# Third layer of a fused fp32 network: rotary key columns as a narrow fp32 product in column quarters, and a first group of two key units and a query unit

## The chip, the cores and the metric

The kernel runs on one core of a Trainium2 chip, as one launch. The metric is device time in microseconds (us) of one execution. Engines are named as the profile names them: PE (TensorE matmul), PEld (its weight load), DVE (VectorE), ACT (ScalarE), POOL (GpSimd), SP (SyncE, which issues nearly all loads).

## The reference, cut to what matters

Three transformer-like layers over 256 latent and 256 context tokens of width 1024, all in fp32. The change lies in the mixer of the third layer, a latent attention. Its projections are:

```
c_q, c_kv, k_pe = split(h @ w_in, [768, 768 + 256])        # w_in: 1024 x 1056
q  = (rms_norm(c_q, q_norm_w) @ w_uq).reshape(b, l, 16, 64 + 32)
kv = (rms_norm(c_kv, kv_norm_w) @ w_ukv).reshape(b, l, 16, 64 + 64)
k_pe = apply_rope_2(k_pe[:, :, None, :], cos, sin)          # latent tokens only
k  = concatenate([k_nope, broadcast_to(k_pe, (b, l, 16, 32))], -1)
```

`c_kv` (256 columns) and `k_pe` (32 columns, the rotary key, the same for all 16 heads) are needed for all 512 tokens, `c_q` (768 columns) for the 256 latent tokens alone. `h` is the modulated norm of the layer's input.

## The kernel before, in words

**Weights.** Weights stream through three slots as units; a unit of this stage is 128 output columns by 1024 inputs (8 blocks k of 128), 512 KB. SP loads it into `raw` (L502; the slot must have been split by POOL), ACT rounds it to fp32r in `w_hi` (L1466; the products of the unit three before must be done), POOL writes the rest `raw - w_hi` to `w_lo` in two halves (L2010). A product of an fp32 weight and an fp32 input is then three fp32r matmuls: high by high, high by low, low by high (`three`, L584 to L586). The list of phases (`weight_phases`) fixes the order of units, steps and banks for every engine; each engine walks it by its own program and waits on counters: `rounded`, `split`, `steps` (PE finished a unit), `taken` (a result was read, so that its PSUM bank is free; the banks rotate over three).

**The third layer's start.** DVE and ACT make `h` block by block: DVE scales (L2230), ACT shifts and rounds (`h_hi`, L1539, counter `h_round`), DVE writes the rest (`h_lo`, L2239, counter `h_split`). Phase `ckv` has three units: two of `c_kv` and a third that holds the 32 rotary columns four times over, so that they fill 128. `linear(..., gate, early=True)` runs the three units side by side over blocks 0 to 3, those products that need only `h_hi` first (L767, L768), the rest after `h_split` (L772), then each unit alone over blocks 4 to 7 (L584 to L586). All have 512 token columns.

**Then.** Phase `cq`: six units with 256 token columns, `high_then_low` (L731, L732, then L737). After its first unit PE waits for `lk_in` and sums the squares of `c_kv` (L1348): ACT squared both key units (L1934), DVE scaled them (L2971) and added the squares (`std`, L2975). After its third unit PE spreads the inverse (L1354). DVE copies the rotary unit to `kpe` (L2103), and turns the latent half with shuffle, two multiplications and an addition (L2979 to L2982). Beside units 1, 2, 4 and 5 of `cq` ACT copies `kpe` to four of the sixteen heads each (L1959). DVE splits `ckv` into high and low (L2106), counter `lk_done`, for which PE waits before phase `uk`: two units of 512 columns by 256 inputs, eight products of six matmuls, each read by two copies of DVE (L2103). Phases `uv` (eight products) and `uq` (twelve units) follow, then attention.

Of the kernel before, what the change touches and what calls it, by code (L numbers as in the profile page):

```python
# [9 lines left out]
F32 = mybir.dt.float32  # L10
# [3 lines left out]
P = 128  # L14
D = 1024
KD = D // P
CTX = LAT = 256
TOK = CTX + LAT
# [20 lines left out]
LQ = LN + LR  # L39
# [96 lines left out]
def weight_phases():  # L136
    out = []

    def ffn(n):
        out.append(Phase(f"up{n}", 2 * KF, KD * P))  # L140
        out.append(Phase(f"down{n}", 3 * KD, SLOT, parts=3))

    out.append(Phase("va_gates", 2, LEAD + KD // 2 * 144))
    out.append(Phase("ka", 1, KD * P))
    out.append(Phase("qa", 4, KD * P))
    out.append(Phase("vma", 2, KD * P, 2, 2))
    out.append(Phase("km", 4, KD * P))
    out.append(Phase("vmb", 2, KD * P, 2, 2))
    out.append(Phase("qm", 4, KD * P))
    out.append(Phase("om", 4, KD * P))  # L150
    out.append(Phase("out0", 8, KD * P))
    ffn(0)
    out.append(Phase("in1", 24, KD * P))
    out.append(Phase("vra", 3, 272, ranges=((0, 3), (3, 6), (6, 8))))
    out.append(Phase("vrb", 2, KD * P, 2, 2))
    out.append(Phase("out1", 8, KD * P))
    ffn(1)
    out.append(Phase("ckv", 3, KD * P))
    out.append(Phase("cq", 6, KD * P))
    out.append(Phase("uk", 2, 2 * 512, 4, 4))  # L160
    out.append(Phase("uv", 2, 2 * 512, TT, TT))
    out.append(Phase("uq", 12, 6 * P))
    out.append(Phase("out2", 8, KD * P))
    ffn(2)
    unit = step = taken = 0
    ada = 16
    for f in out:
        f.every, f.number = CARRIED.get(f.name, (1, 0))
        f.first_ada, f.carry = ada, CARRY.get(f.name, f.units)
        ada += f.carry // f.every * f.number  # L170
        f.first_unit, f.first_step, f.first_taken = unit, step, taken
# [18 lines left out]
def build(nc, dram, small_at, tables_at, layers=3):  # L190
# [4 lines left out]
    with ExitStack() as stack:  # L195
# [296 lines left out]
        @block.sync  # L492
        def _(sp):
            sp.dma_start(small[:, :], dram["small"]).then_inc(s["small_in"], 16)

            def load(g):

                f, u = all_units[g]
                if g >= SLOTS:
                    f0, u0 = all_units[g - SLOTS]  # L500
                    sp.wait_ge(s["split"], 2 * (f0.first_unit + u0 + 1))
                sp.dma_start(raw_slot(f, u), source(f, u)).then_inc(full[g % SLOTS], 16)  # L502
                if g >= SLOTS and f0.every < SLOTS:
                    load_carried(f0, u0)
                if f.every >= SLOTS:
                    load_carried(f, u)

            def load_ada(k):

                if k - 16 >= SLOTS:  # L510
                    sp.wait_ge(s["ada_sum"], sums_after[k - SLOTS + 1])
                sp.dma_start(ada_w[:, k % SLOTS, :], dram[f"ada{k // 48}"][k % 48]).then_inc(ada_full[k % SLOTS], 16)

            def load_carried(f, u):

# [12 lines left out]
            sp.dma_start(X[:, :, 0:L0], dram["ctx"]).then_inc(s["x_in"], 16)  # L528
            sp.dma_start(fixed[:, :], dram["table3"]).then_inc(s["fixed_in"], 16)
            load_first_ada(3, 8)  # L530
            g = 0
            for name in run:
                f = ph[name]
                if name == "qm":

                    sp.wait_ge(s["cond_ready"], 1)
                    sp.dma_start(cond[:, :, :], dram["cond1"]).then_inc(s["cond_in"], 16)
                for u in range(f.units):
                    load(g)
                    if g == 1:  # L540
                        load_first_ada(8, 16)
                    if g == 2:
                        sp.dma_start(room0, dram["table0"]).then_inc(s["tables_in"], 16)
                        sp.dma_start(cond[:, 0, :], dram["cond0"][:, 0, :]).then_inc(s["cond_in"], 16)
                    g += 1

            if layers < 3:
                sp.wait_ge(s["x_ready"], 1)
                if layers == 2:
                    sp.wait_ge(s["taken"], ph["ckv"].first_taken)  # L550
                sp.dma_start(dram["out"], X[:, :, L0:L1]).then_inc(s["out_done"], 16)
                sp.wait_ge(s["out_done"], 16)
            else:
                for n, a in ((0, 2), (1, 4), (None, 0), (2, 6)):
                    if n is None:
                        sp.wait_ge(s["pool_scaled"], 4)
                    else:
                        sp.wait_ge(s["x_ready"], 2 + n)
                    sp.dma_start(dram["out"][:, a:a + 2, :], X[:, a:a + 2, L0:L1]).then_inc(s["out_done"], 16)
                sp.wait_ge(s["out_done"], 64)  # L560
# [3 lines left out]
        def _(pe):  # L564
# [778 lines left out]
            def latent_keys(u):  # L1343
# [7 lines left out]
                if u == 2:  # L1351
# [3 lines left out]
                                         ident, start=True, stop=True)  # L1355
                    last.then_inc(s["lk_spread"], 1)

            def latent_queries():
                pe.wait_ge(s["lq_in"], 1)
                for i in range(2):  # L1360
                    last = pe.matmul(bank[7][:, i:i + 1], sq_sum[:, i * P:(i + 1) * P], ones[:, 0:1],
                                     start=True, stop=True)
                last.then_inc(s["lq_sum"], 1)
# [47 lines left out]
            if layers == 2:  # L1411
                return
            feature_sums(0, TOK, "ckv")
            linear("ckv", 0, TOK, gate=next_h(), early=True)
            linear("cq", L0, L1, after=latent_keys)
            pe.wait_ge(s["lk_done"], 1)

            f = ph["uk"]
# [31 lines left out]
        def _(act):  # L1450
# [486 lines left out]
            def query_parts(u):  # L1937
# [13 lines left out]
                if u == 3:  # L1951
                    for i in range(2):
                        act.wait_ge(s["lk_work"], i + 1)
                        act.activation(ckv_hi[:, i, :], ckv[:, i, :], ACT.Copy).then_inc(s["lk_hi"], 1)
                if u == 1:
                    act.wait_ge(s["kpe_in"], 1)
                if u in (1, 2, 4, 5):
                    q = (1, 2, 4, 5).index(u)
                    act.activation(kh[LN:LQ, 4 * q:4 * q + 4, :], kpe[LN:LQ, :].unsqueeze(1).to_broadcast([LR, 4, TOK]),  # L1959
                                   ACT.Copy).then_inc(s["kpe_done"], 1)  # L1960

# [19 lines left out]

            phase("ckv", key_squares)
            phase("cq", query_parts)
            phase("uk", query_scale)
            phase("uv")
            phase("uq", spread_queries)
            attention(att2, 2 * AH, LH, LQ ** -0.5, False)
            out_and_squares("out2", L0, L1)
# [107 lines left out]
        def _(dve):  # L2096
# [868 lines left out]
            def mixer2():  # L2965
                def keys(p, b):

                    if p == 2:
                        return copy(kpe[LN:LQ, :], b[LN:LQ, :])
                    dve.wait_ge(s["lk_sq"], p + 1)  # L2970
                    return dve.tensor_scalar(ckv[:, p, :], b[:, :], S("kv_norm")[:, p:p + 1], None, ALU.mult)  # L2971

                each_product("ckv", keys)
                taken("cq")
                dve.tensor_tensor(std[:, :], work[:, 0, :], work[:, 1, :], ALU.add).then_inc(s["lk_in"], 1)  # L2975
                dve.wait_ge(s["tables_in"], 48)
                cs, sn = (C2(x) for x in ("cos", "sin"))
                k_lat, k_swap = kpe[LN:LQ, L0:L1], kswap[LN:LQ, :]
                then(dve.stream_shuffle(k_swap, k_lat, swap16))  # L2979
                dve.tensor_tensor(k_lat, k_lat, cs[LN:LQ, :], ALU.mult)  # L2980
                then(dve.tensor_tensor(k_swap, k_swap, sn[LN:LQ, :], ALU.mult))
                dve.tensor_tensor(k_lat, k_lat, k_swap, ALU.add).then_inc(s["kpe_in"], 1)  # L2982

                def queries(p, b):

# [31 lines left out]
                    if p == 0:  # L3017
                        last.then_inc(s["taken"], 1)
                dve.wait_ge(s["lq_lo"], 6)
                taken("uk")  # L3020
                dve.nop().then_inc(s["lq_in"], 1)

                def plain_keys(p, b):

# [158 lines left out]
def _layout(i):  # L3183
# [42 lines left out]
        arrays[f"up{n + 1}"] = _units(_pairs(i["w_ffn_gate_2"][n], i["w_ffn_up_2"][n]), P)  # L3226
        arrays[f"down{n + 1}"] = _units(i["w_ffn_down_2"][n], P)
    arrays["cq"] = _units(w2[:, :768], P)
    arrays["ckv"] = _units(np.concatenate([w2[:, 768:1024], np.tile(w2[:, 1024:], (1, 4))], 1), P)
    uq = np.asarray(i["mla_w_uq_2"][0]).reshape(768, LH, LQ)  # L3230
    arrays["uq"] = _units(np.concatenate([uq[:, :, LN:].reshape(768, -1), uq[:, :, :LN].reshape(768, -1)], 1), P)
    ukv = np.asarray(i["mla_w_ukv_2"][0]).reshape(256, LH, LN + LV)
# [27 lines left out]
```

## Time and profile before

| | us |
|---|---|
| median of 3 runs | 1456.79 |
| lowest, highest | 1455.14, 1459.68 |
| span of the profiled execution | 1454.6 |

The profiled execution's own time is given by its span, from the first instruction to the last. In the profile's page each engine has a line of busy time; a view of stretches gives busy time and granted clock by stage; a timeline gives each instruction's start and duration, with the idle time before it and what ended it. Ends of matmuls are modelled, so the time that one costs in a stream is read from start to start.

### The profile page before, as it was taken

To read this page: it belongs to the slowest core of one execution; us is meant where nothing else is said; L and a number is where in the kernel's file an instruction comes from. 1 tells how busy PE (TensorE), PEld (TensorE's weight loads), DVE (VectorE), ACT (ScalarE), POOL (GpSimd) and SP (SyncE) were. 2 spreads that over 40 slices of the span, in tenths; PEclk is the share of its full clock that TensorE was granted. 3 is DMA by queue.
4 is the path that set the end of the run, shared out by engine and by line. 5 is a ranking of instruction groups with operands and counts; after the bars stand their busy time and mean duration, and the time that the engine had idled before them with its cause. 6 is when DMAs were issued, how large, how long until landed. Compare 5 with 4: busy or idle time off the path is not lost.

```text
span 1454.6 us, 21621 instructions
## 1 busy us (share of the span) xinstructions
PE 1403.6 (96%) x8272; PEld 1172.3 (81%) x8272; DVE 848.5 (58%) x1638; ACT 659.0 (45%) x1070; POOL 840.2 (58%) x672
## 2 busy tenths in 40 slices
PE   5999999999999999999999999999999999999998
PEld 2978789999988888546878888888888866888887
DVE  3798667776676689688675333321126768554522
ACT  3555665455453133684342232232226386544442
POOL 1533427998864444675444554544446530699997
PEclk9999999999999999999999999999999999999999
DMA  9748516777775652010445555533333320365664
GB/s 365 288 164 309 195 50 212 248 258 241 243 259 194 202 192 80 31 44 15 174 174 182 195 202 185 193 122 96 102 107 102 110 94 16 118 200 188 187 187 135
DMA packets 71207, 242.01 MB, mean 166 GB/s; under 512 B 7488, under 2 KB 12992, under 8 KB 70720
## 3 DMA queue, kind: packets, MB, share of 16 engines
q1 hardware_dynamic: 68688, 236.63, 48.1%
q10 hardware_dynamic: 2416, 4.00, 0.9%
q8 instruction: 66, 1.08, 0.3%
q14 instruction: 37, 0.30, 0.1%
HBM read 238.50 MB, written 1.05 MB: 165 GB/s over the span
## 4 chain that ended last, share of the span: by engine, by line
PE 52%; DVE 4%; ACT 1%; issue 0%; POOL 0%; DVEq 0%; ACTq 0%
PE bank L731 9%; PE bank L737 9%; PE bank L732 9%; PE bank L593 8%; PE bank L594 4%; PE bank L584 2%; PE bank L586 1%; PE bank L585 1%; PE bank L592 1%; PE cond_a L1124 1%; PE bank L1124 1%; DVE h_both L2239 1%; PE bank L1132 1%; PE cond_a L1185 1%; PE bank L1144 1%; PE cond_b L1144 1%
## 5 line engine op out<-in xcount | busy, mean ns | idle before, releaser
L2010 POOL TENSOR_TENSOR w_lo<-raw,w_hi 128x512 fp32r<-128x512 f32 (+2 forms) x610 | 776.8, 1302 | 581.1 <-ACT w_hi L1466 572.9
L1466 ACT ACTIVATE w_hi<-raw 128x1024 fp32r<-128x1024 f32 (+3 forms) x300 | 307.9, 1029 | 582.7 <-PE bank L737 375.2
L731 PE MATMUL bank<-h_both,w_hi 128*128 128x512 f32 (+1 forms) x1000 | 323.1, 340 | 1.2 <-ACT w_hi L1466 1.2
L732 PE MATMUL bank<-h_both,w_hi 128*128 128x512 f32 (+1 forms) x1000 | 322.5, 340 | 0.0
L731 PEld LDWEIGHTS bank<-h_both,w_hi 128*128 128x128 f32 x1000 | 188.3, 188 | 22.9 <-ACT w_hi L1466 1.4
L732 PEld LDWEIGHTS bank<-h_both,w_hi 128*128 128x128 f32 x1000 | 188.3, 188 | 21.3
L737 PE MATMUL bank<-h_both,w_lo 128*128 128x512 f32 (+1 forms) x1000 | 198.1, 340 | 0.0
L737 PEld LDWEIGHTS bank<-h_both,w_lo 128*128 128x128 f32 x1000 | 160.4, 188 | 21.4 <-POOL w_lo L2010 0.2
L2124 DVE CUSTOM_DVE_ANT_0 ada_junk<-ada_w,cond_a 128x1024 bf16<-128x1024 f32 x128 | 153.5, 1215 | 15.1 <-DVE work L2687 8.1
L2106 DVE TENSOR_TENSOR hidden_both<-work,hidden_both 128x256 fp32r<-128x256 f32 (+1 forms) x66 | 58.5, 886 | 135.0 <-ACT hidden_both L1547 135.0
L593 PE MATMUL bank<-h_both,w_hi 128*128 128x512 f32 x345 | 122.8, 394 | 0.0
L2674 DVE SCALAR_TENSOR_TENSOR X<-bank,mod,X 128x256 f32<-128x256 f32 x64 | 29.3, 480 | 141.5 <-PE bank L737 123.4
L731 PE MATMUL bank<-hidden_both,w_hi 128*128 128x256 f32 (+1 forms) x330 | 102.7, 331 | 0.0
L732 PE MATMUL bank<-hidden_both,w_hi 128*128 128x256 f32 (+1 forms) x330 | 102.6, 331 | 0.0
L594 PE MATMUL bank<-h_both,w_lo 128*128 128x256 f32 x345 | 96.5, 280 | 0.0
L2124 DVE CUSTOM_DVE_ANT_0 ada_junk<-ada_w,cond_b 128x1024 bf16<-128x1024 f32 x64 | 77.8, 1215 | 0.0
L593 PEld LDWEIGHTS bank<-h_both,w_hi 128*128 128x128 f32 x345 | 64.8, 188 | 13.3 <-issue 0.4
L584 PE MATMUL bank<-h_both,w_hi 128*128 128x256 f32 (+1 forms) x192 | 67.2, 350 | 3.8 <-DVE h_both L2239 1.8
L2103 DVE TENSOR_SCALAR arena<-bank 128x512 f32<-128x512 f32 (+3 forms) x65 | 38.7, 598 | 51.6 <-PE bank L737 33.5
L732 PEld LDWEIGHTS bank<-hidden_both,w_hi 128*128 128x128 f32 x330 | 62.1, 188 | 6.0
L731 PEld LDWEIGHTS bank<-hidden_both,w_hi 128*128 128x128 f32 x330 | 62.1, 188 | 6.0
L594 PEld LDWEIGHTS bank<-h_both,w_lo 128*128 128x128 f32 x345 | 64.9, 188 | 2.0
(487 smaller groups left out, 2544.1 us busy)
## 6 DMA issues: line engine op xcount, KB each, us to landing
raw<-in_up SPq DMA_DIRECT2D x132, 512.0 KB, 3.6
ada_w<-in_ada SPq DMA_DIRECT2D x128, 512.0 KB, 4.5
raw<-in_down SPq DMA_DIRECT2D x48, 448.0 KB, 3.5
raw<-in_out SPq DMA_DIRECT2D x24, 512.0 KB, 3.5
raw<-in_down SPq DMA_DIRECT2D x24, 512.0 KB, 3.6
raw<-in_in SPq DMA_DIRECT2D x24, 512.0 KB, 3.5
arena<-in_ada SPq DMA_DIRECT2D x16, 512.0 KB, 11.8
raw<-in_uq SPq DMA_DIRECT2D x12, 384.0 KB, 3.1
```

The source lines that it names most:

```text
L584: pe.matmul(out, w_h, x_h, start=first, stop=False)
L593: pe.matmul(out.rearrange("p (h n) -> p h n", h=2), w_h, x_both, start=first, stop=False)
L594: return pe.matmul(out[:, 0:LAT], w_l, x_both[:, 0], start=False, stop=False)
L731: pe.matmul(out, w_h[:, k - k0], hi[:, k, cols], start=(k == 0), stop=False)
L732: pe.matmul(out, w_h[:, k - k0], lo[:, k, cols], start=False, stop=False)
L737: last = pe.matmul(out, w_l[:, k - k0], hi[:, k, cols], start=False, stop=(k == K - 1))
L1466: act.activation(part_slot(w_hi, f, u), raw_slot(f, u), ACT.Copy).then_inc(s["rounded"], 1)
L2010: pool.tensor_tensor(part_slot(w_lo, f, u)[:, a:b], raw_slot(f, u)[:, a:b], part_slot(w_hi, f, u)[:, a:b].bitcast(F32), ALU.subtract).then ...
L2103: return dve.tensor_scalar(out, in_, 1.0, None, ALU.mult)
L2106: return dve.tensor_tensor(out, x, hi.bitcast(F32), ALU.subtract)
L2124: dve.tensor_tensor_reduce(ada_junk[:, ada_sums[0] % 2, :], ada_w[:, k % SLOTS, :], silu_c[m][:, :], 1.0, 0.0, ALU.mult, ALU.add, mod[:, n ...
L2674: last = dve.scalar_tensor_tensor(out=X[:, k, a:e], in0=b[:, a - t0:e - t0], scalar=mod[:, layer[0] % 2, 8 * chunk + k, m:m + 1], in1=X[:, ...
```

## The change

- The rotary columns leave phase `ckv` (now two units) and become a phase `kpe` of their own after `cq`: one unit of 1024 by 32, 128 KB. The number of units in all, and each unit's slot from `cq` on, stay: `cq` moves up one place, and `kpe` takes the place before `uk`.
- `latents_first` replaces `linear("ckv")` and the first unit of `cq`: the two key units (512 token columns) and the first query unit (256) run side by side over blocks 0 to 3, each block behind `h_split`, then each alone over blocks 4 to 7; after it `latent_keys(0)`, so the wait for `lk_in`.
- `rotary_keys`, after the last query unit: 32 matmuls in plain fp32 with the unrounded weight in `raw` and both parts of `h`. A result of 32 columns takes a quarter of the array; the four quarters hold context and latent tokens, each for blocks 0 to 3 and for blocks 4 to 7.
- DVE: the copy of the rotary unit and the rotation leave their place before the query units; behind the last query unit it makes four copies of 32x256 out of the bank, adds the halves, and rotates (`rotary_key`), before the copies of `uk`.
- ACT: the copies of `kpe` to the heads move from `cq` to `uv`, two to each of its two units.
- SP: the load of the unit three after `kpe` (the first of `uv`) waits also for the product of `kpe`, which reads `raw`.

```
-    out.append(Phase("ckv", 3, KD * P))
+    out.append(Phase("ckv", 2, KD * P))
     out.append(Phase("cq", 6, KD * P))
+    out.append(Phase("kpe", 1, KD * LR))
...
                     sp.wait_ge(s["split"], 2 * (f0.first_unit + u0 + 1))
+                    if f0.name == "kpe":
+                        sp.wait_ge(s["steps"], f0.steps_after(u0))
...
+            def latents_first(gate):
+                f, n = ph["ckv"], ph["ckv"].units + 1
+                slots = [[part_slot(x, f, u, KD) for x in (w_hi, w_lo)] for u in range(n)]
+                def one(u, k):
+                    t0 = 0 if u < f.units else L0
+                    return three(bank_of(f.first_taken + u)[:, 0:TOK - t0], *(w[:, k] for w in slots[u]),
+                                 h_hi[:, k, t0:], h_lo[:, k, t0:], k == 0, k == KD - 1)
+                for k in range(KD // 2):
+                    gate(k)
+                    for u in range(n):
...
+                        one(u, k)
+                for u in range(n):
+                    for k in range(KD // 2, KD):
+                        if u == 0:
+                            gate(k)
+                        last = one(u, k)
+                    last.then_inc(s["steps"], 1)
+                latent_keys(0)
+            def rotary_keys():
...
+                w = raw_slot(f, 0).rearrange("p (k n) -> p k n", k=KD)
+                for k in range(KD // 2):
+                    for x in (h_hi, h_lo):
+                        for g in range(4):
+                            j, t0 = g // 2 * KD // 2 + k, g % 2 * L0
+                            last = pe.matmul(bank_of(f.first_taken)[LR * g:LR * g + LR, 0:L0], w[:, j],
+                                             x[:, j, t0:t0 + L0].bitcast(F32), start=(k == 0 and x is h_hi),
+                                             stop=(k == KD // 2 - 1 and x is h_lo))
+                last.then_inc(s["steps"], 1)
...
-            linear("ckv", 0, TOK, gate=next_h(), early=True)
-            linear("cq", L0, L1, after=latent_keys)
+            latents_first(next_h())
+            linear("cq", L0, L1, after=latent_keys, first=1)
+            rotary_keys()
             pe.wait_ge(s["lk_done"], 1)
...
+            def spread_rotary_keys(u):
+                act.wait_ge(s["kpe_in"], 1)
+                for q in range(2 * u, 2 * u + 2):
                     act.activation(kh[LN:LQ, 4 * q:4 * q + 4, :], kpe[LN:LQ, :]...
...
+                def rotary_key():
...
+                    copy(kpe[LN:LQ, 0:L0], b[0:LR, 0:L0])
+                    copy(kpe[LN:LQ, L0:L1], b[LR:2 * LR, 0:L0])
+                    copy(rope_s[LN:LQ, 0, :], b[2 * LR:3 * LR, 0:L0])
+                    copy(rope_s[LN:LQ, 1, :], b[3 * LR:P, 0:L0]).then_inc(s["taken"], 1)
...
+                    dve.tensor_tensor(kpe[LN:LQ, 0:L0], kpe[LN:LQ, 0:L0], rope_s[LN:LQ, 0, :], ALU.add)
+                    then(dve.tensor_tensor(k_lat, k_lat, rope_s[LN:LQ, 1, :], ALU.add))
...
                 dve.wait_ge(s["lq_lo"], 6)
-                taken("uk")
+                taken("kpe")
                 dve.nop().then_inc(s["lq_in"], 1)
+                rotary_key()
```

## Rows read from the trace of the kernel before

**Rows 1.** The page: PE's busy time, share of the span and instructions.
```profile
PE 1403.6 (96%) x8272; PEld 1172.3 (81%) x8272; DVE 848.5 (58%) x1638; ACT 659.0 (45%) x1070; POOL 840.2 (58%) x672
```

**Rows 2.** The view of stretches, around the third layer's projections.
```profile
core 0: us, PE busy (x) PEld busy (x) DVE busy (x) ACT busy (x) POOL busy (x), PEclk, DMA share, GB/s
1107.85:1124.10 16.25, 16.25 (x138) 16.12 (x136) 10.18 (x15) 13.86 (x21) 13.55 (x11) 1.00 0.47 160
1125.30:1137.00 11.70, 11.66 (x50) 8.82 (x50) 10.72 (x17) 4.80 (x6) 6.40 (x5) 1.00 0.35 104
1137.30:1148.60 11.30, 11.30 (x50) 9.12 (x50) 7.58 (x14) 1.68 (x3) 3.98 (x4) 1.00 0.24 76
```

**Rows 3.** Timeline of PE: start, duration, what, idle time before and what ended it.
```profile
1087.40 0.50 PE L767 MATMUL bank<-h_both,w_hi 128*128 128x512 f32 x1 [0.33 <-ACT h_both L1539]
...
1099.51 0.40 PE L584 MATMUL bank<-h_both,w_hi 128*128 128x512 f32 x1
...
1104.97 0.28 PE L731 MATMUL bank<-h_both,w_hi 128*128 128x256 f32 x1
...
1107.85 0.95 PE L1348 MATMUL cond_a<-fixed,std 128*128 128x1 f32 x8
...
1123.05 1.12 PE L737 MATMUL bank<-h_both,w_lo 128*128 128x256 f32 x8
1125.34 0.50 PE L584 MATMUL bank<-ckv_hi,w_hi 128*128 128x512 f32 x1 [1.17 <-DVE ckv_lo L2106]
```

**Rows 4.** Timeline of DVE.
```profile
1087.38 0.88 DVE L2239 SCALAR_TENSOR_TENSOR h_both<-cond_b,mod,h_both 128x256 fp32r<-128x256 f32 x2
1096.79 1.87 DVE L2239 SCALAR_TENSOR_TENSOR h_both<-cond_b,mod,h_both 128x256 fp32r<-128x256 f32 x4
1104.16 0.75 DVE L2971 TENSOR_SCALAR spare<-bank,small 128x512 f32<-128x512 f32 x1 [1.96 <-ACT work L1934]
1105.90 0.85 DVE L2975 TENSOR_TENSOR std<-work 128x512 f32<-128x512 f32 x1
1106.78 0.45 DVE L2979 STREAM_SHUFFLE spare<-spare 32x256 f32<-32x256 f32 x1
1108.10 1.50 DVE L2981 TENSOR_TENSOR spare<-spare,arena 32x256 f32<-32x256 f32 x1
1127.66 0.51 DVE L3010 TENSOR_TENSOR sq_sum<-sq_sum,work 128x256 f32<-128x256 f32 x1
1128.34 11.33 DVE L2103 TENSOR_SCALAR arena<-bank 64x512 f32<-64x512 f32 x16 [0.18 <-DVE sq_sum L3010]
1151.02 0.42 DVE L3040 TENSOR_TENSOR spare<-bank,arena 128x256 f32<-128x256 f32 x1 [1.51 <-PE bank L737]
1151.36 0.41 DVE L3041 TENSOR_TENSOR spare<-bank,arena 128x256 f32<-128x256 f32 x1
```

**Rows 5.** Timeline of PE near the kernel's start: fp32 products in column quarters.
```profile
21.91 0.64 PE L661 MATMUL cond_b<-arena 128*32 128x256 f32 x8 [0.25 <-DMA arena<-in_ada]
32.44 1.08 PE L661 MATMUL cond_b<-arena 128*32 128x256 f32 x16
```

**Rows 6.** Timeline of ACT.
```profile
1102.51 1.06 ACT L1466 ACTIVATE w_hi<-raw 128x1024 fp32r<-128x1024 f32 x1 [1.20 <-PE bank L586]
1103.48 0.58 ACT L1934 ACTIVATE work<-bank 128x512 f32<-128x512 f32 x1
1113.60 1.91 ACT L1959 ACTIVATE arena<-spare 32x2048 f32<-32x2048 f32 x1
```

**Rows 7.** Timeline of POOL, and the page's row of a load.
```profile
1106.37 5.82 POOL L2010 TENSOR_TENSOR w_lo<-raw,w_hi 128x512 fp32r<-128x512 f32 x4 [0.17 <-ACT w_hi L1466]
1138.15 1.99 POOL L2010 TENSOR_TENSOR w_lo<-raw,w_hi 128x384 fp32r<-128x384 f32 x2 [2.92 <-ACT w_hi L1466]
...
raw<-in_uq SPq DMA_DIRECT2D x12, 384.0 KB, 3.1
```

**Rows 8.** The view of stretches, after an idle PE; then PE's timeline before one.
```profile
659.80:663.10 3.30, 3.30 (x13) 1.04 (x9) 3.27 (x7) 1.03 (x1) 3.30 (x4) 0.50 0.01 2
...
658.71 2.67 PE L1185 MATMUL bank<-arena,spare 128*64 128x512 f32 x8 [2.10 <-DVE arena L2900]
```

More of the change, by code:

```diff
@@ L1356, in latent_keys @@
                     last.then_inc(s["lk_spread"], 1)
+            def latents_first(gate):
[8 more added lines that the diff above has]
+                    for u in range(n):
+                        if k == 0:
+                            pe.wait_ge(s["split"], 2 * (f.first_unit + u + 1))
+                            room(f.first_taken + u)
+                        one(u, k)
[7 more added lines that the diff above has]
+            def rotary_keys():
+                f = ph["kpe"]
+                loaded(pe, f, 0)
+                room(f.first_taken)
+                w = raw_slot(f, 0).rearrange("p (k n) -> p k n", k=KD)
[7 more added lines that the diff above has]
+                last.then_inc(s["steps"], 1)
             def latent_queries():
@@ L1954, in query_parts @@
                         act.activation(ckv_hi[:, i, :], ckv[:, i, :], ACT.Copy).then_inc(s["lk_hi"], 1)
[L1955 to L1958, printed above, removed]
+            def spread_rotary_keys(u):
+                act.wait_ge(s["kpe_in"], 1)
+                for q in range(2 * u, 2 * u + 2):
                     act.activation(kh[LN:LQ, 4 * q:4 * q + 4, :], kpe[LN:LQ, :].unsqueeze(1).to_broadcast([LR, 4, TOK]),
@@ L1983, in _ @@
             phase("cq", query_parts)
+            phase("kpe")
             phase("uk", query_scale)
-            phase("uv")
+            phase("uv", spread_rotary_keys)
             phase("uq", spread_queries)
@@ L2966, in keys @@
                 def keys(p, b):
-                    if p == 2:
-                        return copy(kpe[LN:LQ, :], b[LN:LQ, :])
                     dve.wait_ge(s["lk_sq"], p + 1)
@@ L2975, in mixer2 @@
                 dve.tensor_tensor(std[:, :], work[:, 0, :], work[:, 1, :], ALU.add).then_inc(s["lk_in"], 1)
-                dve.wait_ge(s["tables_in"], 48)
-                cs, sn = (C2(x) for x in ("cos", "sin"))
[L2978 to L2982, printed above, removed]
+                def rotary_key():
+                    f = ph["kpe"]
+                    product_in(f, 0)
+                    b = bank_of(f.first_taken)
+                    copy(kpe[LN:LQ, 0:L0], b[0:LR, 0:L0])
+                    copy(kpe[LN:LQ, L0:L1], b[LR:2 * LR, 0:L0])
+                    copy(rope_s[LN:LQ, 0, :], b[2 * LR:3 * LR, 0:L0])
+                    copy(rope_s[LN:LQ, 1, :], b[3 * LR:P, 0:L0]).then_inc(s["taken"], 1)
+                    dve.wait_ge(s["taken"], f.first_taken + 1)
+                    k_lat, k_swap = kpe[LN:LQ, L0:L1], kswap[LN:LQ, :]
+                    dve.tensor_tensor(kpe[LN:LQ, 0:L0], kpe[LN:LQ, 0:L0], rope_s[LN:LQ, 0, :], ALU.add)
+                    then(dve.tensor_tensor(k_lat, k_lat, rope_s[LN:LQ, 1, :], ALU.add))
+                    dve.wait_ge(s["tables_in"], 48)
+                    then(dve.stream_shuffle(k_swap, k_lat, swap16))
+                    dve.tensor_tensor(k_lat, k_lat, cs[LN:LQ, :], ALU.mult)
+                    then(dve.tensor_tensor(k_swap, k_swap, sn[LN:LQ, :], ALU.mult))
+                    dve.tensor_tensor(k_lat, k_lat, k_swap, ALU.add).then_inc(s["kpe_in"], 1)
+                cs, sn = (C2(x) for x in ("cos", "sin"))
                 def queries(p, b):
@@ L3228, in _layout @@
     arrays["cq"] = _units(w2[:, :768], P)
-    arrays["ckv"] = _units(np.concatenate([w2[:, 768:1024], np.tile(w2[:, 1024:], (1, 4))], 1), P)
+    arrays["ckv"] = _units(w2[:, 768:1024], P)
+    arrays["kpe"] = _units(w2[:, 1024:], LR)
     uq = np.asarray(i["mla_w_uq_2"][0]).reshape(768, LH, LQ)
```

## The prediction

> **What bounds the kernel now.** I read the page first: PE is busy for 96% of the span [rows 1], so time is won by PE work removed or by its waits removed, and lost by new waits. Then the view of stretches, for the part that changes [rows 2]: in the query units PE is busy throughout, in the key products (`uk`) nearly so, at the full granted clock. Then the timeline of PE [rows 3], to see where each unit starts and the one real wait, 1.17 us before `uk` for DVE's `ckv_lo`; and those of DVE, ACT and POOL [rows 4, 6, 7], since a shorter PE path asks for their results earlier. What the reader should see there is that `uk` is already paced by DVE: its sixteen copies take 11.33 us [rows 4], 1.42 a product, while PE could do a product in 1.40: the 48 matmuls of the same width in `uv` take 11.3 us [rows 2], and the same number in `uk` takes 11.7.
>
> **The price of one matmul.** From 1099.51 to 1104.97 PE runs 24 matmuls of 512 columns, two half units [rows 3], so 0.2275 us each. From 1104.97 to 1107.85 it runs 24 of 256 columns, 0.120 each. A unit of `cq` costs 2.88, a unit with 512 columns 5.46.
>
> **Part 1, the first group.** It no longer starts on `h_hi` alone. Before, PE began at 1087.40 [rows 3]; now it waits for the first `h_lo`, at 1088.26 [rows 4]. A block of the new group costs 6 x 0.2275 + 3 x 0.120 = 1.725, four make 6.9, so PE is at 1095.2, then has 0.68 per block of the first unit. The last block's `h_lo` ends at 1096.79 + 1.87 = 1098.66 in both kernels [rows 4], and that sets the end of the first unit: about 1099.5 before and after. Cost 0; the cover is DVE's pace. If it were gone, the later start would cost 0.9.
>
> Then the second key unit's half, 12 x 0.2275 = 2.73, to 1102.24, and the query unit's half, 12 x 0.120 = 1.44, to 1103.68. Before, PE came to this point (the sums of L1348) at 1107.85 [rows 3]. So 4.17 us go: 2.73 of rotary work ahead of it, and 1.44 of the query unit that now hide behind `h`. (The rotary unit's other half, before, was in the shared stretch; it goes behind DVE's pace and frees nothing there.)
>
> **Part 2, what is late next.** The sums need `lk_in`. ACT rounds a unit when the second key unit is done, at 1102.51, then squares (done 1104.06) [rows 6]; DVE scales from 1104.16 for 0.75 [rows 4]; then, without the rotary copy that stood between, the addition of 0.85 ends at 1105.8. None of these can start earlier, since the second key unit ends when it did. PE therefore sits idle from 1103.7 to 1105.8, a new wait of 2.1 us, and of the 4.17 only 2.05 are kept. Behind that wait stand all other query units. They run on as before: 16.15 us from 1107.85 to 1124.0 [rows 2, 3], now 1105.8 to 1121.95. Weights are no bound there: ACT loses four copies of 1.91 [rows 6], 7.6 us of the 13.9 it was busy in this stretch, and POOL has a unit fewer to split.
>
> **Part 3, the narrow product.** The kernel has the same form at its start: four fp32 products of 128x256 into four column quarters are 8 records, and they take 0.64 us alone and 1.08 for two such sets [rows 5], so 0.44 a set and 0.20 for the tail. Here are 4 blocks x 2 parts = 8 sets: 3.52 us, to 1125.47, with a result at 1125.7. The wait for `lk_done` is gone by then: without ACT's copies and the rotation on DVE, `ckv_lo` follows the fourth query unit, at about 1119.4, and even at its 3.5 us is done by 1123. So `uk` may start at 1125.5, against 1125.34: PE's work is 5.46 less 3.52, but nearly all that is spent by the wait of part 2.
>
> **Part 4, DVE behind it.** The rotation now starts with the result, 1125.75, and DVE's copies of `uk` are queued behind it. An operation of this size with one operand in PSUM takes 0.42, started 0.34 after the one before [rows 4]: four copies are 1.44. The two additions, two multiplications and last addition are like the 0.51 of L3010, 0.40 where the next needn't wait: 2.3. The shuffle is 0.45 [rows 4], own waits some 0.2. Sum 4.4, so the first copy of `uk` starts at 1130.15 and not at 1128.34 [rows 4]: 1.8 later. With three banks PE's fourth product waits for DVE's first, so at 1125.5 + 4.2 PE stops for about 1.9, and from there both kernels go at DVE's 1.42 a product. `uk` ends 1.8 later.
>
> Bounds: at 0.34 for each of the ten operations and 0.45 for the shuffle it is 3.9 (and the shift 1.3); with the 1.50 of L2981 [rows 4] for the five that read two operands in SBUF, some 5 more. That row was measured beside POOL's 5.82 us of splitting [rows 7]. Here POOL is between jobs: its split of the second `uk` unit ends near 1126.2, and the next needs the load held back by part 5. I take the low end. The Trainium skill (SBUF — State Buffer, "Who interferes with whom") says the same as a rule: a DVE instruction with two SBUF inputs and a GpSimd instruction that reads SBUF exclude each other for their whole length. By it a meeting would cost up to 1.4 per instruction; the trace bears that out, and it is a rival below.
>
> **Part 5, the moved edges.** SP's load of the first `uv` unit waits for 1125.7; 3.6 us of DMA at most, 1.06 of ACT [rows 6], 2.6 of POOL: 1133, and `uv` starts at 1139. Behind it in SP's queue stands the second `uv` unit, needed 5.6 later still. Cost 0, cover 6 us. ACT's copies in `uv`: two after the first unit's rounding, two after the second's, 3.82 each, so ACT is free at about 1155.2 where its next rounding could start at 1152.7. PE wants that unit (the fourth of `uq`) at 1157.0, its low part at 1158.5; rounding gives 1156.1, POOL (1.99 a unit [rows 7]) 1158.1. From there load 3.1, rounding 0.85 and split 1.99 make 6.1 for three units where PE takes 6.4. Cost 0, but by a few tenths; if it fails, up to 1.
>
> **Sum.** -2.05 (kept of part 1) + 3.52 (product) - 1.34 (the old wait, 1124.0 to 1125.34) = +0.15 at the start of `uk`; in `uk` the shift of DVE's start decides: +1.8. The profiled execution would go from 1454.6 to 1456.4; the median of the runs shown is 2.2 above that span, so 1458.6.
>
> **The rivals.**
> - *The clock falls at the new wait.* The granted clock is 0.50, so 1.2 GHz of 2.4, over the 3.3 us from 659.8, and PE had been idle 2.10 just before [rows 8]; it did not fall behind the 1.17 before `uk` [rows 2, 3]. Now 2.1 idle is followed by 0.8 of one-column sums [rows 3]. Half speed for such a stretch is 1.65 more: 1460.3. The Trainium skill (TensorE: Matmul & The Clock Gate, "What's actually happening") has the clock halved by too little activity, and by that rule the trace agrees. Against: PE is full on both sides of the new wait, which it isn't around 659.8. Chance 18%.
> - *Not slower: DVE does not decide `uk`.* If copies and rotation behind the product fit in the 2.8 us that PE's first two products leave, PE runs `uk` in 11.2 from 1125.5 and loses nothing; it ends 0.3 earlier than before: 1456.5. It decides from a chain of 2.8 us down. Four copies alone are 1.44 and seven more steps would have to take 0.2 each; every row says more. A shorter wait in part 2 would help the same way. 13%.
> - *POOL meets the rotation.* Two or three blocked instructions, 1.0 each: +3, 1461.6. 8%.
> - *The change doesn't do what it says: the quarters run one after another.* 64 records at 0.22 are 14.1 instead of 3.5: 1469. The sets of [rows 5] speak against it, and the form is the same. 4%.
> - Forecast: 50%. The remaining 7% is anything else, of both signs.
>
> **How the numbers follow.** Time is that of the forecast, 1458.6, with its own range 1457 to 1460.5. Medians of three scatter by more than a microsecond (1455.14 to 1459.68 here); with the rivals the range is 1454.7 to 1462. 0.3%, about what a measurement of this kernel can tell from no change, is 4.4 us: forecast, clock and not-slower lie within it, so within 81%, slower 14% (quarters, half of the POOL case, part of the clock's), faster 5%: even the full 2.05 + 1.34 without any price for the product would be only 3.4.
>
> **What would show it.** An idle of about 2 us before L1348's sums, ended by DVE's `std`; 64 records of the narrow product in 3.7 us; no wait for `ckv_lo`; one wait of about 1.9 in `uk` before its fourth product, with DVE's rotation ahead of its first copy; no idle in `uq`. Wrong if the wait in `uk` is missing, if the sums start before 1105, or if `uq` shows gaps.

## The result, and the profile after

Nine executions of each kernel: the changed one takes 1464.07 us (median, 1460.51 to 1466.35), the one before 1456.79 (1451.40 to 1460.30). The ratio is 1.0047 with a 95% interval of 1.0034 to 1.0059: slower by 0.47%, about 7 us, where I forecast 1.8 and a range up to 1462. Two executions of all that follow, one of before at 1990 us and one of the kernel of experiment 4 at 7876 us, stand far apart from the rest and enter no ratio. The profiled execution has a span of 1462.8, 8.2 more than before. Line numbers have moved: L1351 is what L1348 was, L587 to L589 were L584 to L586, L734, L735 and L740 were L731, L732 and L737.

Timeline of PE after (start, duration, what, idle before it and what ended it):

```profile
1089.07 0.50 PE L587 MATMUL bank<-h_both,w_hi 128*128 128x512 f32 x1 [1.24 <-DVE h_both L2285]
...
1107.52 1.87 PE L1351 MATMUL cond_a<-fixed,std 128*128 128x1 f32 x8 [2.90 <-DVE std L3019]
...
1126.81 3.66 PE L1396 MATMUL bank<-h_both,raw 128*32 128x256 f32 x64
1130.40 0.50 PE L587 MATMUL bank<-ckv_hi,w_hi 128*128 128x512 f32 x1
...
1136.23 0.50 PE L587 MATMUL bank<-ckv_hi,w_hi 128*128 128x512 f32 x1 [1.38 <-DVE arena L2149]
...
1186.52 0.66 PE L1135 MATMUL bank<-fixed,arena 128*128 128x128 f32 x4 [2.30 <-DVE arena L2630]
```

Four places answer to the four steps forecast. There is a new wait before the sums (2.90, not 2.1); the narrow product is 64 records in 3.66; the wait before `uk` [rows 3] is gone; and a wait of 1.38 stands before the fourth product of `uk`. But the sums themselves take 1.87 where they took 0.95 [rows 3]. The view of stretches says why:

```profile
core 0: us, PE busy (x) PEld busy (x) DVE busy (x) ACT busy (x) POOL busy (x), PEclk, DMA share, GB/s
1103.90:1107.10 3.20, 0.72 (x7) 0.52 (x5) 2.13 (x2) 2.52 (x5) 2.99 (x4) 1.00 0.46 148
1107.30:1114.00 6.70, 6.48 (x30) 6.48 (x31) 0.56 (x2) 0.17 (x1) 2.52 (x2) 0.50 0.33 102
1114.20:1126.80 12.60, 12.60 (x107) 12.47 (x105) 6.34 (x13) 7.18 (x14) 7.88 (x8) 1.00 0.29 83
```

PE is busy for 0.72 of the first 3.2 us, and then has a granted clock of 0.50, 1.2 GHz, for 6.8 us. In slices of a tenth of a microsecond the fall stands between 1107.2 and 1107.3, so while PE was still idle, before the sums; the sums and the first query unit behind them then run at the lower clock. Before, the same work ran at 1.00 [rows 2]. Timeline of DVE after:

```profile
1104.94 0.75 DVE L3015 TENSOR_SCALAR spare<-bank,small 128x512 f32<-128x512 f32 x1 [1.97 <-ACT work L1978]
1105.72 1.74 DVE L3019 TENSOR_TENSOR std<-work 128x512 f32<-128x512 f32 x1
...
1124.04 1.29 DVE L2152 TENSOR_TENSOR ckv_lo<-spare,ckv_hi 128x512 fp32r<-128x512 f32 x2 [0.87 <-PE bank L740]
...
1130.54 1.73 DVE L2149 TENSOR_SCALAR spare<-bank 32x256 f32<-32x256 f32 x4 [0.86 <-PE bank L1396]
1132.30 0.42 DVE L3032 TENSOR_TENSOR spare<-spare 32x256 f32<-32x256 f32 x1
...
1134.34 0.42 DVE L3038 TENSOR_TENSOR spare<-spare 32x256 f32<-32x256 f32 x1
1134.79 11.34 DVE L2149 TENSOR_SCALAR arena<-bank 64x512 f32<-64x512 f32 x16
```

The addition behind which the sums wait takes 1.74 and not the 0.85 of before [rows 4]; the chain behind the narrow product takes 4.25 from first copy to the first copy of `uk`, where I had 4.4. Timeline of POOL around the addition, before and then after:

```profile
1103.65 2.54 POOL L2010 TENSOR_TENSOR w_lo<-raw,w_hi 128x512 fp32r<-128x512 f32 x2 [0.19 <-ACT w_hi L1466]
...
1104.43 5.39 POOL L2056 TENSOR_TENSOR w_lo<-raw,w_hi 128x512 fp32r<-128x512 f32 x4 [0.21 <-ACT w_hi L1510]
```

Before, the addition started 2.25 us into a split of 2.54 (1105.90); after, it starts 1.29 into one of 5.39 (1105.72), where POOL goes from its first half of a unit to the second. Timeline of ACT after, in `uv` and `uq`:

```profile
1156.19 3.71 ACT L2004 ACTIVATE arena<-spare 32x2048 f32<-32x2048 f32 x2
1159.93 1.58 ACT L1510 ACTIVATE w_hi<-raw 128x768 fp32r<-128x768 f32 x2
...
1165.84 0.85 ACT L1510 ACTIVATE w_hi<-raw 128x768 fp32r<-128x768 f32 x1 [3.28 <-DMA raw<-in_uq]
```

ACT is late behind the moved copies and then waits for loads; the first turned product of attention waited 2.30, at the place where before it waited 1.66.

Where the 8.2 us of the two profiled executions stand, measured as the shift of the same instruction between them (before to after); the last column is the forecast's shift up to that point:

| up to | shift, us | of it new | forecast, total |
|---|---|---|---|
| the shared stretch (DVE's work at 1090) | +0.8 | +0.8, ahead of all changed work | 0 |
| the sums (1107.85 to 1107.52) | -0.3 | -1.1 | -2.05 |
| start of `uk` (1125.34 to 1130.40) | +5.1 | +5.4 | +0.15 |
| the copies of `uk` on DVE (1128.34 to 1134.79) | +6.5 | +1.4 | +1.8 |
| attention's first turned product (1179.43 to 1186.52) | +7.1 | +0.6 | +1.8 |
| the end | +8.2 | +1.1 | +1.8 |

### The profile page after: what moved, and what is told of

The parts are those of the page before. It is cut to its first block, busy times and chain, and to the rows that moved or that the text cites. A ratio compares the mean times of both kernels' runs of the same rounds, so it can differ in the third digit from the quotient of the medians.

```text
span 1462.8 us, 21708 instructions
## 1 busy us (share of the span) xinstructions
PE 1407.6 (96%) x8312; PEld 1174.9 (80%) x8312; DVE 848.6 (58%) x1643; ACT 657.5 (45%) x1070; POOL 836.8 (57%) x672
## 4 chain that ended last, share of the span: by engine, by line
PE 48%; DVE 4%; POOL 2%; ACT 2%; DMA 1%; issue 1%; DVEq 0%; ACTq 0%
PE bank L734 9%; PE bank L735 9%; PE bank L740 9%; PE bank L596 7%; PE bank L597 3%; POOL w_lo L2056 2%; PE bank L587 1%; PE bank L589 1%; PE bank L588 1%; PE bank L1127 1%; PE cond_a L1127 1%; DVE h_both L2285 1%; PE bank L595 1%; PE cond_a L1188 1%; PE bank L1135 1%
## 5 line engine op out<-in xcount | busy, mean ns | idle before, releaser
L734 PE MATMUL bank<-h_both,w_hi 128*128 128x512 f32 (+1 forms) x992 | 321.7, 342 | 1.2 <-ACT w_hi L1510 1.2
L735 PE MATMUL bank<-h_both,w_hi 128*128 128x512 f32 (+1 forms) x992 | 321.1, 341 | 0.0
L734 PEld LDWEIGHTS bank<-h_both,w_hi 128*128 128x128 f32 x992 | 187.7, 189 | 22.8 <-ACT w_hi L1510 1.4
L735 PEld LDWEIGHTS bank<-h_both,w_hi 128*128 128x128 f32 x992 | 187.7, 189 | 21.3
L740 PE MATMUL bank<-h_both,w_lo 128*128 128x512 f32 (+1 forms) x992 | 197.1, 341 | 0.0
L740 PEld LDWEIGHTS bank<-h_both,w_lo 128*128 128x128 f32 x992 | 159.6, 189 | 21.4 <-POOL w_lo L2056 0.2
L735 PE MATMUL bank<-hidden_both,w_hi 128*128 128x256 f32 (+1 forms) x330 | 102.3, 331 | 0.0
L734 PE MATMUL bank<-hidden_both,w_hi 128*128 128x256 f32 (+1 forms) x330 | 102.3, 331 | 0.0
L587 PE MATMUL bank<-h_both,w_hi 128*128 128x256 f32 (+1 forms) x204 | 71.9, 352 | 4.9 <-DVE h_both L2285 3.0
L589 PE MATMUL bank<-h_both,w_lo 128*128 128x256 f32 (+1 forms) x204 | 68.7, 337 | 0.0
L588 PE MATMUL bank<-h_both,w_hi 128*128 128x256 f32 (+1 forms) x204 | 68.7, 337 | 0.0
L735 PEld LDWEIGHTS bank<-hidden_both,w_hi 128*128 128x128 f32 x330 | 62.0, 188 | 6.1
```

What stands on the lines that cost most here:

```text
L587: pe.matmul(out, w_h, x_h, start=first, stop=False)
L588: pe.matmul(out, w_h, x_l, start=False, stop=False)
L589: return pe.matmul(out, w_l, x_h, start=False, stop=last)
L734: pe.matmul(out, w_h[:, k - k0], hi[:, k, cols], start=(k == 0), stop=False)
L735: pe.matmul(out, w_h[:, k - k0], lo[:, k, cols], start=False, stop=False)
L740: last = pe.matmul(out, w_l[:, k - k0], hi[:, k, cols], start=False, stop=(k == K - 1))
```

## The experiments

All ratios are to the kernel before; kernels of one group (1 to 4; 5, 7 and the first forms of 6 and 8; the second forms of 4, 6 and 8) ran on one chip with the same runs of before. The changed kernel's own ratio comes from another group, so a difference to it is one between two ratios. Here is the theory after the result: **A**, the new wait costs twice, by its idle time and by the lower clock behind it; **A'**, ACT's late copies cost something too. The rivals are named with each run.

**1. The wait filled.** Three unused products ahead of the wait:

```
+                idle(bank[7], 3 * P, 3 * P, 3 * P)
                 latent_keys(0)
```

> The changed kernel, with three extra fp32 products of 128x384 on PE (results unused) just ahead of the wait for lk_in. They take about 1.9 us of an idle 2.9, so if only the idle time counted they'd change nothing. Theory A (the new wait costs twice: its idle time and a fall of the clock to 0.50 for 6.8 us behind it, about 3.1 us of lost work): the granted clock stays 1.0 through the query units, the sums of L1348 take 0.8 and not 1.87, and the kernel is 3 us faster than the changed one, so about 4 slower than before (ratio 1.0030). Rival B (the clock's fall is a chance of the profiled execution and the time goes elsewhere): no difference from the changed kernel, 7 us slower than before (ratio 1.0047).

Measured: 1461.50 us, ratio 1.0037 (1.0023 to 1.0051). In its timeline of PE the idle is 0.97 and the sums are short again; in its view of stretches the clock holds:

```profile
1106.32 2.10 PE L583 MATMUL cond_a<-fixed 128*128 128x384 f32 x6
1109.38 1.05 PE L1351 MATMUL cond_a<-fixed,std 128*128 128x1 f32 x8 [0.97 <-DVE std L3020]
...
1129.32 0.50 PE L587 MATMUL bank<-ckv_hi,w_hi 128*128 128x512 f32 x1
```

```profile
1109.40:1116.00 6.60, 6.60 (x55) 6.60 (x56) 1.27 (x4) 1.87 (x4) 3.66 (x4) 1.00 0.33 102
```

PE has 55 records in this time where it had 30. From the sums to `uk` it takes 19.94 us (1109.38 to 1129.32), in the changed kernel 22.88 (1107.52 to 1130.40), so the clock cost 2.9; the sums come as late in both, 19.4 us behind DVE's first `h_lo`. The mean granted clock over the executions says that this was no chance of the profiled one: 0.9935 before (24 executions), 0.9897 in the changed kernel (9), 0.9932 in five of the six with the wait filled. The sixth stands apart, at 0.942 and 1465.13 us, and nothing here explains it. The ratio alone decides nothing: its interval holds both 1.0030 (A) and 1.0047 (B). It is the clock and the stretch that tell the theories apart, and by them B falls.

**2. The sums one query unit later.**

```
-                latent_keys(0)                    # end of latents_first
-            linear("cq", L0, L1, after=latent_keys, first=1)
+            linear("cq", L0, L1, after=lambda u: latent_keys({1: 0, 2: 2}.get(u, 1)), first=1)
```

> The changed kernel, with the sums of the key squares (and their wait for lk_in) one query unit later, so that 2.88 us of PE work stand ahead of the wait. Theory A: idle 2.9 and clock loss 3.1 both go, 6 us faster than the changed kernel, so 1 slower than before (ratio 1.0007); the wait in uk for DVE's rotation (1.4 to 1.9) stays. Rival B: only the idle 2.9 goes, 4.4 slower than before (ratio 1.0030). Rival C (the wait merely moves, because ACT and DVE are late by as much): no gain at all, 1.0047.

Measured: 1457.08, ratio 1.0005 (0.9993 to 1.0016): 6.1 us of the 7 are back, as A had it (1.0007); B's 1.0030 and C's 1.0047 lie outside the interval. Timeline of PE, then the view of stretches:

```profile
1104.26 1.05 PE L1351 MATMUL cond_a<-fixed,std 128*128 128x1 f32 x8
...
1164.22 0.36 PE L734 MATMUL bank<-cq_hi,w_hi 128*128 128x256 f32 x1 [1.02 <-ACT arena L2022]
1178.28 0.66 PE L1135 MATMUL bank<-fixed,arena 128*128 128x128 f32 x4 [1.86 <-DVE arena L2629]
```

```profile
1104.30:1121.00 16.70, 16.70 (x172) 15.29 (x176) 7.57 (x16) 8.95 (x18) 13.24 (x12) 1.00 0.36 104
1179.10:1182.40 3.30, 3.30 (x7) 1.84 (x8) 1.77 (x5) 1.67 (x4) 0.00 (x0) 0.50 0.36 129
```

No idle before the sums. But now the copies that ACT makes in `uv` show: PE idles 1.02 in `uq` and 1.86 ahead of attention. At attention's start the clock falls too, but that can't be laid to the copies: it falls there in the profiles of 5, the first form of 6 and the second of 8 behind a wait of 1.66 or 1.67, and holds behind the 2.30 of the changed kernel.

**3. The narrow product without the new first group.**

```
-            latents_first(next_h())
-            linear("cq", L0, L1, after=latent_keys, first=1)
+            linear("ckv", 0, TOK, gate=next_h(), early=True)
+            linear("cq", L0, L1, after=latent_keys)
```

> One part alone: the rotary columns as the late fp32 product, but the first group is the two key units only, started on h_hi as before, and all six query units follow whole. PE then has a query unit of 2.88 us ahead of the wait and not half of one (1.44). Theory A (idle and clock): DVE's addition ends at the same time or, without POOL beside it, 0.9 earlier, so about 1 us of idle remains instead of 2.9, the clock doesn't fall, and the kernel is 3 to 4 us faster than the changed one although PE has the same work in all: ratio 1.002 to 1.003. Rival B (the narrow product and what follows it is the cost, not the first group): as the changed kernel, 1.0047.

Measured: 1461.11, ratio 1.0033 (1.0022 to 1.0045), so about 2 us better than the changed kernel and not 3 to 4, with intervals that overlap. Timeline of PE and view of stretches:

```profile
1092.73 0.50 PE L587 MATMUL bank<-h_both,w_hi 128*128 128x512 f32 x1 [0.83 <-DVE h_both L2285]
...
1105.60 1.05 PE L1351 MATMUL cond_a<-fixed,std 128*128 128x1 f32 x8 [1.49 <-DVE std L3019]
```

```profile
1091.10:1094.50 3.40, 1.96 (x7) 0.99 (x7) 3.40 (x10) 1.78 (x5) 0.00 (x0) 1.00 0.00 0
1094.60:1097.90 3.30, 3.17 (x8) 1.98 (x7) 2.19 (x7) 0.84 (x2) 0.00 (x0) 0.50 0.00 0
```

The wait before the sums is 1.49 (half a microsecond over the expected, since the addition takes 1.77 here too) and the clock held there. It fell earlier: with two units only, PE waits for DVE again and again in the shared stretch (busy 1.96 of 3.40 us), and once more at attention's start. So in this profile the query unit in the first group isn't waste: it keeps PE fed there. The late copies cost more here as well: PE idles 1.29 in `uq` and 1.97 ahead of attention.

**4. Later sums, and ACT's copies in the first units of `uk` and `uv`.** As 2, and

```
             def query_scale(u):
+                if u == 0:
+                    spread_rotary_keys(0)
-            phase("uv", spread_rotary_keys)
+            phase("uv", lambda u: spread_rotary_keys(1) if u == 0 else None)
```

> As the kernel with the later sums, and ACT's copies of the rotary key moved from the two units of uv to the first of uk (two) and the first of uv (two), places where ACT stood idle 4.5 us. Theory A': the copies in uv's second unit put ACT's rounding of uq 2.5 us late, and the loads behind it; the first turned product of attention then waited 2.3 for DVE and not 1.66. With the copies earlier this goes: 0.6 to 0.8 faster than the kernel with the later sums, ratio about 1.000. Rival: uq hid the lateness, no difference.

> The kernel with later sums and earlier copies once more, on the chip of the other two. From its profile it should be level with before (0.1 us faster from the shared stretch to attention), ratio 0.9995 to 1.0000; its first measurement gave 0.9989 with an interval from 0.9978 to 1.0001. If it were truly 1.6 us faster, a part of the gain would stand outside the stretch that the change touches.

Measured: 1454.87, ratio 0.9989 (0.9978 to 1.0001); once more on another chip 1455.36, ratio 0.9990 (0.9976 to 1.0003). Timeline of PE:

```profile
1106.53 1.05 PE L1351 MATMUL cond_a<-fixed,std 128*128 128x1 f32 x8
...
1129.44 0.50 PE L587 MATMUL bank<-ckv_hi,w_hi 128*128 128x512 f32 x1 [1.38 <-DVE arena L2150]
...
1179.09 0.66 PE L1135 MATMUL bank<-fixed,arena 128*128 128x128 f32 x4 [1.66 <-DVE arena L2631]
```

Of the new waits only the 1.38 in `uk` is left, and attention's wait is the 1.66 of before. Against 2 it is 2.2 us better, where A' had 0.6 to 0.8; in the two profiles the stretch from `uk` to attention is 1.45 shorter (the table below). Against before, each interval just includes no change, and the stretch itself is level (-0.1 below); if the ratio's 1.5 us are real, they stand outside it.

**5. The changed kernel, with the copies moved alone.** The second edit of 4.

> The changed kernel with one edge undone: ACT's four copies of the rotary key stand in the first unit of uk (two) and the first of uv (two) and not in both units of uv. Theory A' (the late copies held ACT's rounding of uq back, and the loads of three units later with it): the wait at attention's start goes from 2.30 to 1.66 and ACT no longer waits for the loads of uq; 0.7 to 2.3 faster than the changed kernel, so a ratio to before of 1.003 to 1.004, with idle and clock fall at the sums unchanged. Rival: uq hides it, ratio 1.0047.

Measured: 1461.74, ratio 1.0044 (1.0032 to 1.0056), a smaller gain than the 1.003 to 1.004 expected; the clock still falls at the sums, and once more at attention's start. In the timeline of PE attention's wait is 1.66 again, so 0.64 of the +7 is shown in the profile; a gain beyond that appears where PE isn't already late, as in 4. The interval doesn't exclude the rival's 1.0047; the timeline does.

```profile
1105.38 1.64 PE L1351 MATMUL cond_a<-fixed,std 128*128 128x1 f32 x8 [2.90 <-DVE std L3021]
...
1183.87 0.87 PE L1135 MATMUL bank<-fixed,arena 128*128 128x128 f32 x4 [1.66 <-DVE arena L2632]
```

**6. The rotation left out.** As 4, with `return` behind the four copies of the narrow product.

> The kernel with later sums and earlier copies, with the two additions and the rotation behind the narrow product left out (part of the result is not computed: the halves of the rotary keys are not added and not turned). Theory A (DVE's chain behind the product is what makes PE wait in uk, 1.38): without it the wait goes and uk runs at PE's pace, 1.4 to 1.9 faster than the kernel it is made from, ratio to before about 0.9978. Rival (uk is paced by its sixteen copies whatever stands before them): PE's wait falls, but the end of uk moves by under 0.5, ratio 0.9987.

> The same with the additions and the rotation left out (part of the result is not computed), once more beside the kernel that it is made from. Its uk ended 1.7 us earlier in the profile, but the whole didn't measure faster (1.0000 against 0.9989, from two chips). Theory A: on one chip it is 1.7 faster than the kernel it is made from. Rival E (the time is given back later, by more falls of the clock at attention's start, one of which its profile had): under 0.7 faster, and the mean granted clock lower by 0.0005 or more.

Measured: 1456.20, ratio 1.0000 (0.9990 to 1.0009); beside the kernel of 4: 1455.13, 0.9989 (0.9976 to 1.0002) against 0.9990. In both profiles the wait in `uk` is gone and `uv` starts 1.7 us sooner, counted from the group's first product (47.2 instead of 48.9), so A is right about the stretch. The whole isn't measurably faster: the means of the second pair are 1455.0 and 1455.7, with the mean granted clock at 0.9924 and 0.9937. That is what rival E expected; but the clock fell at attention's start in the first profile alone, and with a scatter of 2 to 3 us between executions neither figure proves it. That later falls of the clock take the gain back is possible, not shown.

**7. The kernel before, with the copies moved alone.**

> The kernel before with one edge of the change alone: ACT's copies of the rotary key leave cq for the first units of uk and uv. Theory A': the wait of 1.17 ahead of uk goes, and DVE starts its copies of uk 1.5 to 2 earlier: 1.2 to 1.7 faster than before, ratio 0.9990. Rival (the gain of the kernel with later sums comes from the narrow product and not from this): no difference, 1.0000.

Measured: 1455.77, ratio 0.9997 (0.9985 to 1.0010). In its timeline the wait before `uk` is 0.52 and not 1.17, but not gone as expected: DVE's `ckv_lo` still takes 3.31 for its two halves beside POOL, nearly the 3.47 of before, against 1.29 in the changed kernel:

```profile
1120.29 3.31 DVE L2109 TENSOR_TENSOR ckv_lo<-spare,ckv_hi 128x512 fp32r<-128x512 f32 x2
```

So the gain is about 0.65 us in the profile, not 1.2 to 1.7, and below what the runs resolve.

**8. The narrow product inside the wait.** The first query unit becomes a phase of its own, `kpe` follows it, then the sums and the other five; DVE turns the keys in steps beside units 1 to 3, in the second form 3 to 5.

```
-    out.append(Phase("cq", 6, KD * P))
+    out.append(Phase("cqa", 1, KD * P))
     out.append(Phase("kpe", 1, KD * LR))
+    out.append(Phase("cq", 5, KD * P))
...
+            rotary_keys()
+            latent_keys(0)
+            linear("cq", L0, L1, after=lambda u: latent_keys(u + 1))
```

> A version to beat both: the narrow product stands between the first group and the sums, so that its 3.5 us fill the wait of 2.9 for lk_in; DVE turns the rotary keys in three steps beside the query units; ACT's copies early as above. Worked out from the profiles: sums at 1107.2 where before had 1107.85 (-0.65), no wait ahead of uk (-1.17), uk at PE's pace from its start (-0.4): 2.2 faster than before, ratio 0.9985, with the granted clock at 1.0 throughout the stretch. Rival (DVE, now with eleven more operations beside the query units, is late with the inverse of the key norm or with ckv_lo): a new wait of 1 to 3 before the spread or before uk, ratio 1.000 or above.

> As the kernel with the narrow product in the wait, with DVE's two additions behind the scaling of ckv (query unit 3), shuffle and multiplications behind ckv_lo (unit 4), the last addition behind unit 5. In the first form DVE came to the scaling of ckv at 1122.3, 7 us after the spread, and PE idled 3.42 ahead of uk. Theory D (that queue on DVE, drawn out by POOL's splits, was the cause): the wait ahead of uk is under 0.5, the clock stays at 1.0, uk starts 35.5 us after the first product of the group and not 38.9, and runs in 11.3 to 11.7: 4 to 5 faster than the first form, ratio to before 0.9985 to 0.9995. Rival (SP's load of the third query unit, held back until the narrow product is done, and POOL's backlog behind it, were the cause): a wait of 1 to 3 stays, ratio 1.001 to 1.003.

Measured: 1459.69, ratio 1.0026 (1.0016 to 1.0036), and 1461.46, 1.0034 (1.0021 to 1.0047). The first form's expectation (0.9985) and theory D for the second both fell; even the second's rival, a wait of 1 to 3, was too small. Timelines of PE, POOL and DVE of the second form:

```profile
1105.44 1.05 PE L1352 MATMUL cond_a<-fixed,std 128*128 128x1 f32 x8
...
1126.07 0.80 PE L588 MATMUL bank<-ckv_hi,w_hi 128*128 128x512 f32 x1 [4.20 <-DVE ckv_lo L2156]
```

```profile
1110.33 16.81 POOL L2060 TENSOR_TENSOR w_lo<-raw,w_hi 128x512 fp32r<-128x512 f32 x12 [3.17 <-ACT w_hi L1511]
```

```profile
1119.83 1.42 DVE L3040 TENSOR_TENSOR spare<-spare 32x256 f32<-32x256 f32 x1
1121.17 1.50 DVE L3041 TENSOR_TENSOR spare<-spare 32x256 f32<-32x256 f32 x1
1122.70 3.31 DVE L2156 TENSOR_TENSOR ckv_lo<-spare,ckv_hi 128x512 fp32r<-128x512 f32 x2
```

PE passes the sums without idling, but SP's load behind the narrow product is held until it is done, POOL has nothing to split for 3.17 us and then works through 16.81 without a break; DVE's operations with two operands in SBUF take two to three and a half times as long beside it (1.42 and 1.50 against the 0.42 above, `ckv_lo` 3.31 against 1.29), `ckv_lo` is late, PE idles 4.20 (3.42 in the first form), and the clock falls within that wait, in both forms. Held loads and DVE's queue both stand in this chain; which of them alone would do wasn't separated.

**All profiles over the same stretch.** Ahead of this stretch one execution is several us earlier or later than another (DVE's first `h_lo` starts between 1082.27 and 1089.98 in the thirteen profiles). So here is each kernel from that start to the start of `uk`, and from there to attention's first turned product, one profile each:

| kernel | to `uk` | `uk` to attention | together, against before |
|---|---|---|---|
| before | 37.96 | 54.09 | 0 |
| changed | 42.26 | 56.12 | +6.3 |
| 1, wait filled | 39.34 | 55.56 | +2.9 |
| 2, sums later | 36.50 | 56.94 | +1.4 |
| 3, without the first group | 40.01 | 57.29 | +5.3 |
| 4, sums later, copies early (two profiles) | 36.48, 36.47 | 55.49, 55.47 | -0.1, -0.1 |
| 5, copies early | 42.36 | 55.49 | +5.8 |
| 6, rotation left out (two profiles) | 36.49, 36.48 | 53.76, 53.76 | -1.8, -1.8 |
| 7, before with the copies moved | 37.32 | 54.08 | -0.65 |
| 8, narrow product in the wait (two forms) | 39.84, 40.59 | 55.08, 56.45 | +2.9, +5.0 |

The forecast was 38.1 and 55.7 (before, plus 0.15 and plus 1.65). The second half holds: with the copies early it is 55.5, 1.4 over before, and without the rotation the 1.4 are gone. The first half is where the changed kernel misses, by 4.2. In two cases the stretch lies just outside what the ratio's interval says of the whole (1: +2.9 against 3.4 to 7.4 us; the first of 6: -1.8 against -1.5 to +1.3); for the others it lies inside.

## Why the prediction was wrong

- **Part 1** held: the first group starts later and ends with DVE's pace (the last product of the shared stretch starts 0.8 later, as all of DVE's work does); no cost.
- **Part 2 is the step that failed, by size and by what stands behind it.** The place was right. I let DVE's addition keep its 0.85; it took 1.74, and 1.75 to 1.80 in the kernels of experiments 1 to 4. Before, the rotary copy held it back until POOL's split was nearly done; now it starts 1.0 earlier against POOL. In all eleven profiles without the rotary copy it starts 1.3 into POOL's job and takes 1.74 to 1.80; in the two with it (before and 7) it starts 2.25 into it and takes 0.85. That it waits for POOL is read from these starts; no run took POOL away. The missing copy thus gave nothing, and 1.1 us were kept up to the sums, not 2.05. And "they run on as before: 16.15 us" was wrong: from the sums to the narrow product it took 19.29 (1107.52 to 1126.81), and 16.35 with the wait filled.
- **The clock** I had as a rival with 18% and 1.65 us. It came, stayed down for 6.8 us where I had priced the 3.3 of [rows 8], and cost 2.9. This and the 0.9 of part 2 are 3.8 of the 4.5 us by which the forecast missed in this stretch (+6.3 against +1.8). "PE is full on both sides of the wait" was my argument against it, and it was wrong: the clock fell within the wait itself, in experiment 5 just behind it. Whether it would have fallen at the 2.1 forecast is open: no run has a wait of that length there; at 0.97 and 1.49 it held. I also priced the rivals one at a time, and the range ended at 1462, just above one of them; here the clock and a meeting with POOL came together. None of the signs that I had named for being wrong came up (the wait in `uk` is there, the sums start later than 1105, `uq` has no gap): they watched the parts that held.
- **Part 3** held: 3.66 us for the narrow product (3.52 + 0.20), no wait for `lk_done`.
- **Part 4** held: 1.38 us of waiting in `uk` and a chain of 4.25 (4.4). The five operations with two operands in SBUF took 0.42 each, since POOL was between jobs. The rival with POOL didn't come about here; it came about at part 2, where I hadn't looked for it.
- **Part 5** cost 0.64 in the profile instead of 0, by the edge that I had called good for a few tenths; by experiment 2 against 4 it costs 1.45 in the profile and 2.2 by the medians once PE isn't late from elsewhere.
- The rest is a shift of 0.8 ahead of everything that was changed and 1.1 spread over the last layer. Executions of one kernel differ by 9 us (1451.4 to 1460.3), so this needs no cause of its own, and none was looked for.

The forecast's mechanism alone, the extra price at DVE, is what kernel 4 has left, and there the work saved ahead of it pays for it (-0.1 in the profile, ratios 0.9989 and 0.9990). Kernel 2 has the late copies besides (1.0005); the 0.4% above that is the new wait with its clock, which experiments 1 and 2 show.

## What to carry to other kernels

Work taken from PE ahead of a chain of other engines isn't won, it becomes a wait. Price the wait by when the chain ends, and add what a fall of the clock would cost; here the order in which PE got its work decided 0.4%. Before you trust a duration of a DVE operation with two operands in SBUF, look where it will now stand against POOL's jobs. A margin of a few tenths in a ring of three slots was gone here as soon as something else in the ring came late; it was cheaper to put ACT's copies where ACT stood idle.

## What the runs showed of the hardware

- The granted clock fell to 0.50 within a wait of 2.90 us of PE and stayed there for 6.8 us, in a stretch that was full before and after; in the profile of experiment 5, with the same wait, it fell 0.3 us behind its end. It fell for 3.4 us in the shared stretch of experiment 3, where PE was busy for 1.96 of 3.40 us with waits of 0.83 and 0.61, and it held behind a wait of 1.49 in the same execution.
- The length of a wait alone doesn't tell. At attention's start, behind 1.66 or 1.67 us, the clock fell in three profiles (5, the first of 6, the second of 8) and held in six (before, both of 4, 7, the first of 8, the second of 6); it fell behind 1.86 and 1.97 (2 and 3) and held behind 1.74 and 2.30 (1 and the changed kernel).
- The same fp32 addition of 128x512 on DVE takes 0.85 or 1.74 to 1.80, by where it starts against POOL's split; subtractions of this size (`ckv_lo`) take 0.65 each beside an idle POOL and 1.7 beside a busy one.
- Sets of four fp32 products in column quarters run at 0.45 us a set also where each quarter has its own weights and its own moving data (64 records in 3.66).
